# Two blocks of a hybrid model on one core: the rounded gate halves begin 64 bytes further on

## What is computed

```python
proj = h @ w_in            # first block; h is the normalised input, 256 x 2048
(u_a, q_b, f_b, i_b, og_b, cx_c, v_c, o_c, ig_c, fg_c, gates) = split(proj)
g_a, g_b, g_c = gates[..., :D_MODEL], gates[..., D_MODEL:2 * D_MODEL], gates[..., 2 * D_MODEL:]
# sigmoid of g_a, g_b, g_c weights the three mixers' projected outputs
```

## Time and profile before

| | |
|---|---|
| median of 3 runs | 2983.12 us (2980.38 to 2985.36) |
| span of the profiled execution | 2978.0 us |
| TensorE busy | 2946.2 us (99%), 18616 matmuls |
| weight loads busy | 2630.0 us (88%) |
| VectorE busy | 2051.0 us (69%) |
| ScalarE busy | 1311.7 us (44%) |
| GpSimd busy | 70.0 us (2%) |
| transfers | 530.39 MB, 178 GB/s over the span |
| gate stage | about 300 to 664 us of the span |

### The profile page before, as it was taken

One profiled execution on the slowest core, in us unless ns is written; L12 is line 12 of the kernel. 1 busy time (PEld: TensorE's weight loads), 2 busy tenths in 40 slices (PEclk: granted clock), 3 DMA queues, 4 the chain that ended last, 5 costly groups with the idle time before them and its releaser, 6 DMA issues.

```text
span 2978.0 us, 47097 instructions
## 1 busy us (share of the span) xinstructions
PE 2946.2 (99%) x18616; PEld 2630.0 (88%) x18616; DVE 2051.0 (69%) x2624; ACT 1311.7 (44%) x1418; POOL 70.0 (2%) x72
## 2 busy tenths in 40 slices
PE   8999999999999999999999999999999999999999
PEld 8898898999988888888888888876998888888888
DVE  6675787977788888885557776636666666666444
ACT  5354423444444444444444354425445444444333
POOL 0000000000001000000000000000000000000000
PEclk9999999999999999999999999999999999999999
DMA  6553334555555555555555544531555555555555
GB/s 230 184 183 134 114 120 149 168 173 198 186 196 193 189 196 194 190 182 190 193 195 198 195 172 168 186 122 43 184 198 186 195 197 188 193 197 177 194 193 184
DMA packets 87359, 530.39 MB, mean 178 GB/s; under 512 B 9952, under 2 KB 10336, under 8 KB 41184
## 3 DMA queue, kind: packets, MB, share of 16 engines
q1 hardware_dynamic: 87264, 529.07, 50.7%
HBM read 526.94 MB, written 2.10 MB: 178 GB/s over the span
## 4 chain that ended last, share of the span: by engine, by line
PE 96%; DVE 2%; ACT 1%; DMA 0%; issue 0%; SPq 0%; DVEq 0%; ACTq 0%
PE bank L576 74%; PE late L576 22%; DVE arena L1687 1%; DVE w_low L1687 0%; DVE half_low L1687 0%; DVE arena L1684 0%; ACT w_high L1203 0%; PE late L1144 0%; DVE arena L1989 0%; DMA ring<-in_w_gates 0%; DMA xT<-in_xT 0%; DVE acts_both L1687 0%; DVE arena L2045 0%; DVE arena L2016 0%; DVE xrs L1734 0%
## 5 line engine op out<-in xcount | busy, mean ns | idle before, releaser
L1687 DVE TENSOR_TENSOR w_low<-ring,w_high 128x2048 fp32r<-128x2048 f32 (+1 forms) x480 | 1014.3, 2113 | 384.1 <-ACT w_high L1203 380.2
L1203 ACT ACTIVATE w_high<-ring 128x2048 fp32r<-128x2048 f32 (+1 forms) x480 | 849.5, 1771 | 636.0 <-DMA ring<-in_w_down 223.0
L576 PE MATMUL bank<-up_early,w_high 128*128 128x512 f32 x1408 | 487.8, 389 | 0.0
L576 PE MATMUL bank<-up_late,w_high 128*128 128x512 f32 x1408 | 487.3, 389 | 0.0
L576 PE MATMUL late<-acts_both,w_high 128*128 128x512 f32 x1408 | 479.0, 389 | 0.3 <-DVE w_low L1687 0.3
L576 PE MATMUL bank<-up_early,w_low 128*128 128x256 f32 x1408 | 388.6, 276 | 0.0
L576 PE MATMUL late<-acts_both,w_low 128*128 128x256 f32 x1408 | 388.6, 276 | 0.0
L576 PE MATMUL bank<-up_late,w_low 128*128 128x256 f32 x1408 | 388.6, 276 | 0.0
L576 PEld LDWEIGHTS bank<-up_early,w_high 128*128 128x128 f32 x1408 | 264.5, 188 | 55.2
L576 PEld LDWEIGHTS late<-acts_both,w_high 128*128 128x128 f32 x1408 | 264.3, 188 | 55.1 <-DVE w_low L1687 0.6
L576 PEld LDWEIGHTS bank<-up_late,w_high 128*128 128x128 f32 x1408 | 264.0, 188 | 54.7
(11 more groups left out here) (311 smaller groups left out, 4946.2 us busy)
## 6 DMA issues: line engine op xcount, KB each, us to landing
ring<-in_w_up SPq DMA_DIRECT2D x176, 1024.0 KB, 4.7
ring<-in_w_down SPq DMA_DIRECT2D x128, 704.0 KB, 4.0
ring<-in_w_in SPq DMA_DIRECT2D x66, 1024.0 KB, 4.7
ring<-in_w_mix SPq DMA_DIRECT2D x62, 1024.0 KB, 4.8
ring<-in_w_gates SPq DMA_DIRECT2D x96, 512.0 KB, 3.7
ring<-in_w_branch SPq DMA_DIRECT2D x16, 1024.0 KB, 4.7
ring<-in_w_out SPq DMA_DIRECT2D x16, 1024.0 KB, 4.8
ring<-in_w_o SPq DMA_DIRECT2D x16, 1024.0 KB, 4.8
```

The costliest lines, as they stand in the source:

```text
L576: return nc.tensor.matmul(o, lhsT, rhs, start=first, stop=last)
L1203: A(w_high[:, s, 0:cols], ring[:, s, 0:cols], ACT.Copy).then_inc(rounded[s], 1)
L1687: return V.tensor_tensor(o, a, b, op)
```

## The change

The aliased tensor `half_high` gets 64 bytes more of offset, and a tensor `ring_pad` of 32 floats (128 bytes) in each partition is laid behind the ring, so that the last half, which now ends 64 bytes behind the ring, has room. `xT`, `hT`, the small tensors and the arena thereby begin 128 bytes further on, and the arena is 128 bytes shorter. `half_raw` and `half_low` stay where they were in the ring.

```diff
 GATES, HALF = 48, UNIT // 2
+HALF_SHIFT = 64
 GATES_FED = 46
@@
         ring = sb("ring", [P, RING, UNIT])
         ring_base = nc.sbuf_base - RING * UNIT * 4
+        sb("ring_pad", [P, 2 * HALF_SHIFT // 4])
         xT = sb("xT", [P, KT, T])
@@
         half_low = alias("half_low", ring_base, [P, RING, HALF])
-        half_high = alias("half_high", ring_base, [P, RING, HALF], 2 * UNIT // T)
+        half_high = alias("half_high", ring_base, [P, RING, HALF], 2 * UNIT // T, HALF_SHIFT)
```

## The result

| | before | after |
|---|---|---|
| median | 2983.14 us (2980.38 to 2985.36) | 3025.94 us (3024.0 to 3027.39) |
| span of the profiled execution | 2978.0 us | 3022.2 us |
| ratio of after to before | | 1.0154 [1.0139, 1.0169] |

The account below looks back on a forecast made before the run. TensorE was taken as the bound, matmuls times their start distance. From 2983.1 us, 1328 gate matmuls x (120.0 - 117.8) ns took 2.9 us, all other terms 0, giving 2980.2 us; range 2973 to 2987 us.

Parts of the forecast that it names:

- Step (g): Outside the gates: padding puts w_low 128 bytes off every moving operand; effect taken as 0, the other case kept as rival.
- The third rival: Outside the gates, padding slows each pair from 340.4 to 347 ns: +28 us, 3011 us; chance 0.13.
- the 77,824 bytes of the prediction: Sum of tensor sizes between ring and arena with the pad, 76 x 1024, used to say all start level modulo 1024.
- Step (b): Gate stage: shifted half_high matmuls start 117.8 instead of 120.0 ns apart, 1328 on the path, gaining 2.9 us.
- The second rival: Gate stage: every half_high load costs 113.3 ns as w_high's in the down projection; gain 8.9 us, 2974.2 us; chance 0.27.
- Step (c): Gate stage: half_low's 768 matmuls, now 128 bytes off the moving tile, stay at 120 ns, +-4.5 us.
- (a): Whole kernel: no instruction, semaphore or transfer is added or removed, and no order changes.
- (d): VectorE's subtraction for half_low, 1219 ns: a stagger of its operands changes nothing, 0.
- (e): ScalarE's rounding to half_high, 1058 ns against 1040 for h_high: even the 18 ns don't matter, 0.
- (f): Transfers into the ring land on the same bytes, 0; an earlier free slot only helps at 494.9 us.
- The first rival: Gate stage: nothing moves, since consecutive loads or product order matter; gain 0.5 us or 0, 2982.6 or 2983.1 us; chance 0.20.
- The named sign: First and down projections should keep 117.8 and 340.4 ns; if they move, padding is at work, by up to tens of us.

Follow-up runs that it names:

- pad_only: The kernel before with only the 128 bytes of padding behind the ring, half_high not shifted: 3027.33 us, 1.0164 times the kernel before.
- shift_only: The kernel before with half_high 64 bytes further, xT and hT laid ahead of the ring so moving tiles keep their grid: 2980.92 us, ratio 1.0033.
- pad256: The kernel before with 256 bytes of padding behind the ring and no shift: 2980.46 us, a single time.
- bench: A separate kernel, not the model, with only float32r matmuls over weight offsets in 32-byte steps: one copy alone takes 113.3 to 119.9 ns a matmul.
- all_moved: The kernel before with 128 bytes ahead of the ring, so everything moves together and no distance changes: 2976.38 us, ratio 1.0002.
- halves64: The kernel before with 256 bytes of padding behind the ring and raw, low and high halves all 64 bytes further: 2969.7 us, ratio 0.9964.
- w64: The kernel before with W_SHIFT at 64 instead of 960, so w_high lies 64 bytes past the moving tiles' grid: 3025.59 us, ratio 1.0154.

## Why the prediction was wrong

**Step (g) failed**: "Steps of 128 and 256 aren't in the trace. I take 0". The padding costs 48.3 us in pad_only's profile (3026.3 - 2978.0), 51.4 us when the 3.1 us of the clock in "to up 2", which the kernel before alone has of the two, are left out, and 51.4 us between the medians (3027.33 - 2975.93). It is the whole loss. The third rival had the mechanism, `w_low` 128 bytes off the moving tile, and the right sign, with a chance of 0.13. Its price was half: 6.6 ns a pair was assumed from the slowest known load beside a single matmul (120 ns), and the up projections pay 353 - 340 = 13 ns for their pairs. The start stamps of the first up projection say which part was missing, as means: behind the matmul of 256 columns 113.4 ns became 119.9, as assumed, but behind that of 512 columns 226.7 became 233.4, where the rival had left 227. Their two stages lose 18.6 us each, the down projections 4.5 and 9.4, the second block's inputs 6.4, the out projection 1.7. The first projection gained 4.7 us from the same padding and the gates 3.1, some 0.7 us of which are the transfer at 494.88 us. The argument against that rival, no dependence on steps of 512, was no evidence: the dependence has a period of 256, in which 512 is nothing and 128 is half. Nor could the constant load duration have shown it: the load of `w_low` in the up projections lasts 187 to 191 ns in after, median 188, as for the down projections in the earlier trace rows; the distance of starts changes, the record of a load hardly does:

```profile
L578 PEld LDWEIGHTS bank<-up_early,w_low x1408: 187/188/191, 839.4 to 2767.1; 128*128 128x128 f32 x176
```

The sign that the load of `half_high` should fall from a median of 192 ns to 187 or 188 did come, 188 ns in after. But pad_only, without the shift, has 188 too, so it says nothing for the shift. And the 77,824 bytes of the prediction are the way from the start of the ring to the arena, ring included; nothing hangs on it, since the ring is a multiple of 1024 bytes.

**Step (b) was right in its mechanism.** The forecast was 117.8 ns for `half_high`; after has 353.4 / 3 = 117.8, and shift_only, without the padding, 117.3. But in after 118.8 of it would have come without the shift (pad_only, 356.4 / 3); the shift adds 1.0 ns there and 2.6 ns in shift_only. That the forecast was met to a tenth is luck. The sum of 2.9 us compares with 4.4 us of shift_only's gate stage, about 0.6 us of which are the transfer at 494.88 us, that isn't on its chain. The second rival's price of 113.3 ns does exist, but only once `half_low` is at 64 too.

**Step (c)**: 120 ns was taken for `half_low`. It is 118.8 in after (pad_only: 118.7): the padding moved it, within its bounds, by 1.2 ns to the good. Over the 1328 and 660 matmuls on the path the two paces are worth 1328 x 2.1 + 660 x 1.2 = 3.6 us where 2.9 were forecast. The stage gained 5.4 us, with the 1.6 us of the clock in it. One reading of the path held for the kernel before alone: in after the chain lies on VectorE from 470.0 to 500.6 us, where the kernel before has TensorE and then the transfer; pad256 has it so too.

**Steps (a), (d), (e), (f)** stand. The instructions are the same 18616 matmuls; VectorE's `half_low` takes 1219 ns and its `w_low` 2291 ns, as in the earlier trace rows:

```profile
L1689 DVE TENSOR_TENSOR w_low<-ring,w_high 128x2048 fp32r<-128x2048 f32 x352 | 806.5, 2291 | 190.8 <-ACT w_high L1205 186.7
...
L1689 DVE TENSOR_TENSOR half_low<-ring,half_high 128x1024 fp32r<-128x1024 f32 x96 | 113.8, 1219 | 32.2 <-ACT half_high L1390 31.1
```

The VectorE piece of the gate stage was to keep its length: it ran from 340.35 to 382.23 us, 41.9 us, and now from 333.61 to 375.48, 41.9 us.

```profile
333.61 0.70 DVE arena L1686
...
375.48 5.58 PE bank L578 x32
```

**The first rival**, and with it the rule of the Trainium skill that TensorE's two reads are independent ("SBUF — State Buffer", "Who interferes with whom"), fell, as far as the time of a matmul is concerned: the measurement decides. The same matmul and load take 113.3 or 119.8 ns by the offset alone (bench), and all_moved says that it is the distance of the two, not the address of one. The order of products isn't the cause either: halves64 keeps the order and is at 113 to 114 ns.

**The named sign** worked: "if these move, the padding is at work and the prediction is wrong in (g)". The first projection and the first down projection moved, from 117.8 to 115.7 ns and from 340.4 to 347 ns. What should have been done was to give that case the weight that its reach asked for: the shift touched 1328 matmuls on the path, the padding nearly all of the 18616, and the distance that the padding made, 128 bytes for `w_low`, stood in no row.

## What to carry to other kernels

A change of a tensor's address is a change for every operand that lies behind it. Before padding is added, list the distances between weights and moving tiles modulo 256 bytes in each stage and keep them, by padding in multiples of 256, unless they are what is to be changed. Where a float32r matmul with 256 columns is bound by its start distance, a microkernel over offsets shows in one run what a trace of one placement can't, namely that the offset counts, its period and its best values. The whole kernel has still to be timed: here it paid 353.3 ns for pairs that the microkernel had at 346.6.

## What the runs showed of the hardware

- A 128 x 128 float32r load beside 256 moving columns costs a start distance between 113.3 and 119.9 ns at the granted clock of 1.00, by the offset of weights against moving tile modulo 256 bytes; 768 columns in a mixed stream cost 340 to 360 ns (bench, and the whole kernels within the same bounds; single combinations in bench reach 364). Over the kernel the placement makes 2%, 2963.8 to 3028.6 us in the profiles. What in the memory has this period isn't shown.
- The stream can settle in different rhythms on the same addresses and hold one for a whole stage: 340 or 350 ns a pair in w64's two up projections. The first down projection has it too. pad256 and halves64 have the same distances there, and 246.8 and 240.0 us:

```profile
1344.84 50.17 PE late L577 x287
```
```profile
1344.84 50.32 PE late L577 x296
```

- The 6.8 us between these two is also about the distance between the two clusters in which the times of the kernel before fall on one chip (2973.9 to 2978.7 us and 2982.4 to 2986.8). That the rhythm makes the clusters is argued from the size alone. The clock is a second source of about half that size: the stretch at 0.50 in "to up 2" costs 3.1 us in the kernel before, and pad256, with the same distances, doesn't have it. shift_only has the same wait before that place, for VectorE's 1.86 us, and keeps 1.00; so what makes the clock fall isn't shown. The rhythm would also explain why shift_only, with a shorter gate stage, has no lower median; what starts a rhythm, and why w64's up projections and after's choose the slow one, stays open.
- Why pairs and triples have different best offsets (64 / 0 and 64 / 64) stays open too. The table is measured, not derived.
